# First modulation in quarters of the features instead of halves, with three projections begun beside it

## The chip, the cores and the metric

One Trainium2 chip, one of its cores. The metric is the device time of one execution, in microseconds (us). The engines of the core run side by side and wait for each other through semaphores: TensorE (PE) multiplies matrices, ScalarE (ACT) and VectorE (DVE) work on elements, GpSimd (POOL) does a few side jobs, and SyncE (SP) issues most of the transfers (DMA) from the chip's memory.

## The reference

Three transformer layers over 256 tokens of 1024 features, in float32. The part that matters here is the beginning of the first:

```
mod = (silu(c) @ w_ada + b_ada)          # 6 x 1024: shift1, scale1, gate1, shift2, scale2, gate2
h   = rms_norm(x, norm1_w) * (1 + scale1) + shift1
proj = h @ w_in                          # keys, queries, values of the delta rule, gates a and b, ...
qkv = silu(causal_conv(proj[:, :1536]))  # 4 taps, per feature
```

`c` is one vector, so `silu(c) @ w_ada` is a product of a vector with a matrix of 1024 x 6144. `h` needs its first two parts, shift1 and scale1: 2048 columns, 8 MB of weights. Behind `qkv` stand the gated delta rule, window attention, the output projection, a gated feed-forward layer and two more layers.

## The kernel before

Activations lie with the features on the 128 partitions: `x`, `norm_tmp` and the pair `h_hi`, `h_lo` have 8 pieces ("k", contraction steps) of 128 features by 256 tokens. To keep float32 precision, each operand of a product is split into a high part (ACT, `hi`, L669 and `first_highs`, L718) and a low part (DVE, `lo`, L1072 and `first_lows`, L1185), and every product is three: high x high, high x low, low x high (`three`, L1715). Weights come as blocks of 1 MB, 256 output columns each, from one stream in the order in which they are used, through a ring of three raw buffers (`load`, L548): block n + 3 is fetched when the low part of block n has been made. The column blocks w0 to w5 are the two halves of the keys, of the queries and of the values; a block is 8 steps x 2 tiles x 3 = 48 products.

The first modulation runs in two halves of 512 features each (loop lines 1864 to 1892 on PE). For each half SP loads four matrices of 1 MB (`load_ada`, L557, pieces of 2 KB in memory): scale rows in two, shift rows in two, the last of which comes as two transfers. `ada` (L1827) multiplies a column of `silu(c)` with four 512-wide rows at once in four groups of 32 columns of the PE array; ACT copies the result (`mod_rows_copy`, L713); `row_sums` (L1837) turns each 128 of it into a column and adds over the partitions. The last quarter of each half goes by `last_columns` (L1848) in 64 products of one output column. DVE then makes scale and shift (`first_scales` L1129, `first_shifts` L1135), scales the rows (`first_scaled` L1121), ACT makes `h_hi` (`h_high`, L696), DVE `h_lo` (`first_low` L1125). Beside the loads of the second half PE does steps 0 to 3 of w0 and w1 (`column_half`, L1721, with FIRST_WEIGHTS = 2, L30). `warm` (L1859) issues products of zeros that nobody reads, which fill the PE while it waits.

After the second half `project` (L1917) finishes w0, then come the 24 products for the gates a and b (lines 1928 to 1932, into bank B[0]), the rest of w1, and w2 to w5 whole. For each block ACT copies the product into `pad` (L759) when the convolution of the block before is done, DVE convolves it (L1229 to L1247) and ACT applies silu (`feature`, L743), whose result the next convolution waits for. DVE's order in this loop (L1218) is `lo(w + 2)`, then the convolution of w; ACT's (L750) is `hi(w + 2)`, the copy of w, `feature(w - 1)`. Every engine works strictly in the order in which its program is written, so a wait holds up all that stands behind it.

Later, from L1287 on, DVE alternates between splitting w8 to w10, the sums of the next modulation (`accumulate`) and reading the banks that PE fills (`row_scale`, L1301); PE may fill a bank again when DVE has read it (`before`, L1948).

Of the kernel before, what the change touches and what calls it, by code (L numbers as in the profile page):

```python
# [29 lines left out]
FIRST_WEIGHTS = 2  # L30
# [138 lines left out]
class Semaphores:  # L169


    def __init__(self, new):
# [3 lines left out]
        self.ada_rest_landed = new("ada_rest_landed")  # L176
# [143 lines left out]
def build(nc, stream, x_in, consts_in, vectors_in, gab_in, t5_onehot, t5_log, rel_bias, out):  # L320
    t5_scratch = nc.dram_tensor("t5_scratch", (16, 384), F32, kind="Internal")
    with ExitStack() as ctx:
        s = Semaphores(lambda name: ctx.enter_context(nc.semaphore(name)))
        ada_landed = [ctx.enter_context(nc.semaphore(f"ada_landed{i}")) for i in range(4)]
# [79 lines left out]
        mod_rows = [[inv_b[:, 1024 * i + 512 * u:1024 * i + 512 * u + 512] for u in range(2)] for i in range(2)]  # L404
        ada_raw = [flat(AT), flat(qkT), flat(X), flat(kqb[:, 0:8, :])]
# [140 lines left out]
        @block.sync  # L546
        def _(sp):
            def load(i):  # L548
                if i >= RING:
                    kind, n, _ = LOADS[i - RING]  # L550
                    if kind == "w":
                        sp.wait_ge(s.lo_ready, n + 1)
                    else:
                        sp.wait_ge(s.mod_accumulated, n - MOD_START[1] + 1)
                sp.dma_start(raw[:, i % RING, :], stream[LOADS[i][2]]).then_inc(raw_landed[i % RING], 16)

            def load_ada(half, i):  # L557
                if half and i < 3:
                    sp.wait_ge(s.ada_used, i + 1)
                elif half:  # L560
                    sp.wait_ge(s.rows_summed, 2)
                k, c = 4 * (i % 2), 512 * half + (D if i < 2 else 0)
                rows = ada_raw[i].rearrange("p (k c) -> p k c", k=4)
                if i < 3:
                    sp.dma_start(rows, stream[k:k + 4, :, c:c + 512].rearrange("k p c -> p k c")).then_inc(ada_landed[i], 16)
                    return
                for two, landed in enumerate((ada_landed[3], s.ada_rest_landed)):
                    sp.dma_start(rows[:, 2 * two:2 * two + 2, :],
                                 stream[k + 2 * two:k + 2 * two + 2, :, c:c + 512].rearrange("k p c -> p k c")).then_inc(landed, 16)
# [3 lines left out]
            for i in range(4):  # L573
                load_ada(0, i)
            load(0)
            load(1)
            for i in range(4):
                load_ada(1, i)
            sp.wait_ge(ada_landed[2], 32)
            for i in range(2, len(LOADS)):  # L580
# [73 lines left out]
        def _(act):  # L654
# [58 lines left out]
            def mod_rows_copy(half, u):  # L713

                act.wait_ge(s.ada_used, 3 * half + (3 if u else 2))
                act.activation(mod_rows[half][u], B[u][:, :], ACT.Copy).then_inc(s.rows_copied, 1)
# [12 lines left out]
            first_highs(0, (1,))  # L729
            h_high(0, range(2, 4))  # L730
            first_highs(0, (2, 3))
            first_highs(1, (0, 1))
            act.wait_ge(s.gab_loaded, 16)
            act.activation(gab_wh[:, :], gab_w[:, :], ACT.Copy).then_inc(s.gab_hi, 1)
            first_highs(1, (2, 3))
            mod_rows_copy(1, 0)
            mod_rows_copy(1, 1)
            h_high(0, range(4, KD))
# [11 lines left out]
            for w in range(6):  # L750
                hi(w + 2)
# [10 lines left out]
                if w == 0:  # L762
                    act.wait_ge(s.gab_product, 1)
                    act.activation(gabT, B[0][0:16, 0:T], ACT.Copy).then_inc(s.gab_copied, 1)
# [299 lines left out]
        def _(dve):  # L1064
# [64 lines left out]
            def first_scales(half):  # L1129
                c, at = slice(4 * half, 4 * half + 4), 480 + 8 * half  # L1130
                dve.wait_ge(s.rows_summed, 2 * half + 1)
                link(dve.tensor_tensor(a1[:, c], STAT[:, at:at + 4], b_scale[:, c], ALU.add))
                dve.tensor_tensor(a1[:, c], a1[:, c], vecs("norm1")[:, c], ALU.mult).then_inc(s.mod_ready, 1)

            def first_shifts(half):  # L1135
                c, at = slice(4 * half, 4 * half + 4), 484 + 8 * half
                dve.wait_ge(s.rows_summed, 2 * half + 2)
                dve.tensor_tensor(mods[:, c], STAT[:, at:at + 4], vecs("b_ada")[:, c], ALU.add).then_inc(s.mod_ready, 1)
                dve.wait_ge(s.mod_ready, 2 * half + 2)

            def h_parts_2():
                dve.wait_ge(s.rstd_ready, 2)
                dve.wait_ge(s.mod_ready, 6)
# [17 lines left out]
            def residual(last):  # L1161

                for m in range(KD):
# [4 lines left out]
                    if m == 0:  # L1168
                        dve.wait_ge(s.mod_ready, 5)
# [12 lines left out]
            for k in range(KD):  # L1182
                dve.tensor_tensor(nt[:, k, :], x[:, k, :], B[3][:, 256:512], ALU.mult).then_inc(s.x_scaled, 1)
# [16 lines left out]
            first_scaled(2)  # L1200
            first_scaled(3)
            first_lows(0, (1,))
            first_low(2)
            first_low(3)
            first_lows(0, (2, 3))
            first_lows(1, (0, 1, 2, 3))
            dve.wait_ge(s.gab_hi, 1)
            dve.tensor_tensor(gab_wl[:, :], gab_w[:, :], gab_wh[:, :], ALU.subtract).then_inc(s.gab_lo, 1)
            first_scales(1)
            first_shifts(1)  # L1210
            for k in range(4, KD):
                first_scaled(k)
                if k > 4:
                    first_low(k - 1)
            first_low(KD - 1)


            for w in range(6):  # L1218
# [5 lines left out]
                lo(w + 2)  # L1224
# [479 lines left out]
        def _(pe):  # L1704
# [16 lines left out]
            def column_half(w, bank, ks):  # L1721

                if ks[0] == 4:
                    pe.wait_ge(s.lo_ready, w + 1)
                wh = high_of(w)
                wl = low_of(w)
                for k in ks:
                    if k in (0, 2):
                        pe.wait_ge(s.first_lo, 3 * w + k // 2 + 1)
                    pe.wait_ge(s.h_lo_ready, k + 1)  # L1730
# [96 lines left out]
            def ada(half, i):  # L1827

                pe.wait_ge(ada_landed[i], 16 * (half + 1))
                if half and i % 2 == 0:  # L1830
                    pe.wait_ge(s.rows_copied, 1 + i // 2)
                for k in range(4):
                    ins = mm(B[i // 2][32 * k:32 * k + 32, :], c_columns[:, 4 * (i % 2) + k, :],
                             ada_raw[i][:, 512 * k:512 * k + 512], i % 2 == 0, i > 0)
                ins.then_inc(s.ada_used, 1)

            def row_sums(half, u):  # L1837

                pe.wait_ge(s.rows_copied, 2 * half + u + 1)
                if half + u:  # L1840
                    pe.wait_ge(s.mod_ready, 2 * half + u)
                for j in range(4):
                    at = 480 + 8 * half + 4 * u + j
                    ins = by_halves(STAT[:, at:at + 1], mod_rows[half][u][:, P * j:P * j + P], ones, j == 0, u == 0)
                if u == 0:
                    ins.then_inc(s.rows_summed, 1)

            def last_columns(half):  # L1848

                for k in range(4):  # L1850
                    if k % 2 == 0:
                        pe.wait_ge(s.ada_rest_landed if k else ada_landed[3], 16 * (half + 1))
                    for j in range(4):
                        at = 484 + 8 * half + j
                        ins = by_halves(STAT[:, at:at + 1], ada_raw[3][:, 512 * k + P * j:512 * k + P * j + P],
                                        c_act[:, 4 + k:5 + k], False, k == 3)
                ins.then_inc(s.rows_summed, 1)
# [13 lines left out]
            warm(4)  # L1871
            ada(0, 1)
            warm(3)
            row_sums(0, 0)
            warm(2)
            ada(0, 2)
            warm(3)
            row_sums(0, 1)
            warm(1)
            last_columns(0)  # L1880
            warm(6)
            column_half(0, A[0], range(4))
            ada(1, 0)
            column_half(1, A[1], range(2))
            ada(1, 1)
            column_half(1, A[1], range(2, 4))
            row_sums(1, 0)
            ada(1, 2)
            warm(3)
            row_sums(1, 1)  # L1890
            last_columns(1)
            warm(4)
# [24 lines left out]
            def project(w, halfway=None):  # L1917
                wait_bank(w)
                if w < 2:
                    column_half(w, A[w], range(4, KD))  # L1920
# [3 lines left out]
            for w in range(6):  # L1924
                project(w)
                if w == 0:

                    pe.wait_ge(s.gab_lo, 1)
                    for k in range(KD):
                        a, b = gab_wh[:, 16 * k:16 * k + 16], gab_wl[:, 16 * k:16 * k + 16]  # L1930
                        ins = three(B[0][0:16, 0:T], a, b, h_hi[:, k, :], h_lo[:, k, :], k == 0, k == KD - 1)
                    ins.then_inc(s.gab_product, 1)
# [386 lines left out]
            def spread(f, half):  # L2319

                if f == 0:
                    pe.wait_ge(s.mod_ready, 7)
# [234 lines left out]
```

## Time and profile before

| | us |
|---|---|
| median of 3 runs | 991.35 (990.08 to 991.51) |
| profiled execution | 990.9 |
| its span | 989.1 |
| PE busy | 978.5 (99% of the span) |
| DVE busy | 607.8 (61%) |
| ACT busy | 476.8 (48%) |

The busy time of PE counts a product from its start to its modelled end, so waits of PE that are shorter than a product's way through the array hardly show in it. The page's chain of work that ended last leads back from the end of the kernel to its start, and 98% of it is PE.

### The profile page before, as it was taken

What the parts mean: (1) busy time and instruction counts of PE and PEld (TensorE: products, weight loads), DVE (VectorE), ACT (ScalarE), POOL (GpSimd) and SP (SyncE); (2) the same over time, 40 slices, a digit from 0 to 9 for tenths busy, and PEclk for the clock granted to TensorE, in tenths of its full rate; (3) what the DMA queues carried; (4) which work ended last, traced back from release to release, by engine and by line L of the source; (5) the groups of instructions that cost most, each with busy time, mean ns of one, the idle gap of its engine ahead of it and who ended that gap; (6) DMA issues with size and microseconds to landing.
All of it is one profiled execution on the core that took longest, in us unless ns stands there. A gap on an engine that the chain in (4) does not pass through costs nothing.

```text
span 989.1 us, 15628 instructions
## 1 busy us (share of the span) xinstructions
PE 978.5 (99%) x6703; PEld 847.0 (86%) x6703; DVE 607.8 (61%) x750; ACT 476.8 (48%) x640; POOL 36.8 (4%) x37
## 2 busy tenths in 40 slices
PE   9999999999999999999999999999999999999998
PEld 6799988978888888999888888889999888888886
DVE  2589988775665454787754545365876663545444
ACT  3485277454343435533354344446655563435343
POOL 0000560010000000000000000000000000000000
PEclk9999999999999999999999999999999999999999
DMA  9757324775767354446544645454643435454621
GB/s 345 284 191 259 122 87 151 270 243 214 278 217 285 132 211 172 171 171 214 211 145 153 216 167 206 177 191 153 226 156 130 139 144 185 180 204 166 216 86 43
DMA packets 31588, 185.70 MB, mean 188 GB/s; under 512 B 3040, under 2 KB 5536, under 8 KB 10784
## 3 DMA queue, kind: packets, MB, share of 16 engines
q1 hardware_dynamic: 29984, 180.37, 51.0%
q0 software_dynamic: 832, 3.17, 1.0%
q8 instruction: 53, 0.87, 0.3%
q10 hardware_dynamic: 704, 1.17, 0.3%
q14 instruction: 15, 0.12, 0.0%
HBM read 183.62 MB, written 1.07 MB: 187 GB/s over the span
## 4 chain that ended last, share of the span: by engine, by line
PE 98%; DVE 1%; ACT 0%; issue 0%; POOL 0%; DVEq 0%; POOLq 0%
PE bank L1706 51%; PE acc L1706 43%; PE bank L2308 1%; PE bank L2086 1%; PE bank L1802 0%; PE acc L1802 0%; PE acc L2086 0%; PE bank L2166 0%; PE bank L1979 0%; DVE inv_b L1391 0%; DVE norm_tmp L1511 0%; DVE silu_and_hid L1510 0%; DVE inv_b L1384 0%; PE acc L2316 0%; DVE X_inv L1435 0%
## 5 line engine op out<-in xcount | busy, mean ns | idle before, releaser
L1075 DVE TENSOR_TENSOR w_lo<-raw,w_hi 128x2048 fp32r<-128x2048 f32 x144 | 326.9, 2289 | 146.2 <-ACT w_hi L675 146.1
L1706 PE MATMUL bank<-w_hi,h_parts 128*128 128x512 f32 x1056 | 333.5, 391 | 1.3 <-DVE h_parts L1152 1.3
L675 ACT ACTIVATE w_hi<-raw 128x2048 fp32r<-128x2048 f32 x144 | 271.5, 1909 | 102.3 <-PE acc L1706 70.9
L1706 PEld LDWEIGHTS bank<-w_hi,h_parts 128*128 128x128 f32 x1056 | 198.2, 188 | 44.6 <-issue 2.0
L1706 PE MATMUL bank<-w_lo,h_parts 128*128 128x512 f32 x528 | 205.5, 389 | 0.0
L1706 PE MATMUL acc<-h_parts,w_hi 128*128 128x256 f32 x928 | 170.8, 286 | 0.6 <-DVE h_parts L1127 0.6
L1706 PEld LDWEIGHTS acc<-h_parts,w_hi 128*128 128x128 f32 x928 | 143.5, 190 | 5.3 <-issue 3.3
L1706 PE MATMUL acc<-h_parts,w_lo 128*128 128x256 f32 x464 | 131.2, 283 | 0.0
L1706 PE MATMUL acc<-w_hi,o_hi 128*128 128x512 f32 x296 | 119.1, 402 | 0.0
L1706 PEld LDWEIGHTS bank<-w_lo,h_parts 128*128 128x128 f32 x528 | 99.2, 188 | 19.8
L1706 PE MATMUL acc<-w_hi,o_lo 128*128 128x512 f32 x296 | 115.6, 391 | 0.0
L1706 PE MATMUL acc<-w_lo,o_hi 128*128 128x512 f32 x296 | 115.6, 390 | 0.0
L1706 PEld LDWEIGHTS acc<-h_parts,w_lo 128*128 128x128 f32 x464 | 88.0, 190 | 0.0
L927 ACT ACTIVATE silu_and_hid<-bank,rms 128x256 f32<-128x256 f32 x44 | 20.9, 475 | 105.2 <-PE bank L1706 105.2
L1550 DVE TENSOR_TENSOR o_lo<-bank,o_hi 128x512 fp32r<-128x512 f32 x33 | 22.8, 691 | 76.0 <-ACT o_hi L932 76.0
L1706 PEld LDWEIGHTS acc<-w_hi,o_lo 128*128 128x128 f32 x296 | 55.6, 188 | 12.4
L1706 PEld LDWEIGHTS acc<-w_hi,o_hi 128*128 128x128 f32 x296 | 55.6, 188 | 10.9 <-issue 0.2
L1706 PEld LDWEIGHTS acc<-w_lo,o_hi 128*128 128x128 f32 x296 | 55.7, 188 | 10.5
L932 ACT ACTIVATE o_hi<-bank 128x512 fp32r<-128x512 f32 x33 | 19.8, 599 | 75.2 <-PE bank L2308 75.2
L1542 DVE SCALAR_TENSOR_TENSOR silu_and_hid<-bank,rms,silu_and_hid 128x256 f32<-128x256 f32 x44 | 21.2, 481 | 36.6 <-ACT silu_and_hid L927 36.6
L1706 PE MATMUL bank<-h_parts,w_hi 128*128 128x256 f32 x192 | 34.7, 283 | 0.3 <-DVE h_parts L1520 0.3
L1706 PEld LDWEIGHTS bank<-h_parts,w_hi 128*128 128x128 f32 x192 | 29.4, 188 | 0.7 <-DVE h_parts L1520 0.5
(370 smaller groups left out, 993.3 us busy)
## 6 DMA issues: line engine op xcount, KB each, us to landing
raw<-stream SPq DMA_DIRECT2D x162, 1024.0 KB, 5.1
AT<-stream SPq DMA_DIRECT2D x2, 1024.0 KB, 11.8
qkT<-stream SPq DMA_DIRECT2D x2, 1024.0 KB, 13.0
X_inv<-stream SPq DMA_DIRECT2D x2, 1024.0 KB, 14.2
keys_queries<-stream SPq DMA_DIRECT2D x4, 512.0 KB, 12.4
t_tables<-t_scratch POOLq DMA_DIRECT2D x1, 2048.0 KB, 10.2
x_res<-x_in SPq DMA_DIRECT2D x2, 512.0 KB, 5.2
t_tables<-t_scratch POOLq DMA_DIRECT2D x1, 1024.0 KB, 12.4
```

The source lines that it names most:

```text
L675: act.activation(high_of(w), raw_of(r), ACT.Copy).then_inc(s.hi_ready, 1)
L927: act.activation(sg[:, T * t:T * t + T], B[t][:, 0:256], ACT.Silu, scale=rms[:, t:t + 1] if f else 1.0).then_inc(s.silu_ready, 1)
L932: act.activation(hid_parts(j)[0].rearrange("p a b -> p (a b)"), B[2][:, :], ACT.Copy).then_inc(s.hid_hi_ready, 1)
L1075: dve.tensor_tensor(low_of(w), raw_of(weight_load(w)), high_of(w), ALU.subtract).then_inc(s.lo_ready, 1)
L1542: dve.scalar_tensor_tensor(out=o, in0=up, scalar=rms[:, t:t + 1], in1=gate, op0=ALU.mult, op1=ALU.mult).then_inc(s.hid_ready, 1)
L1550: dve.tensor_tensor(low.rearrange("p a b -> p (a b)"), B[2][:, :], high.rearrange("p a b -> p (a b)"), ALU.subtract).then_inc(s.hid_lo_rea ...
L1706: return pe.matmul(o, l, r, start=start, stop=stop, skip_group_check=True)
L2086: ins = pe.transpose(bank[hh][:, P * i:P * i + P], sc[:, hh, P * i:P * i + P], perm)
L2308: ins = pe.transpose(B[2][:, T * i + P * t:T * i + P * t + P], hid[:, T * t + P * i:T * t + P * i + P], ident)
```

## The change

`load_ada(q, u)` now loads, for each quarter q of 256 features, one matrix of scales (u = 0) and one of shifts (u = 1), each 1 MB in pieces of 1 KB. Blocks w0, w1 and w2 are loaded behind quarters 0, 1 and 2. `ada(q, u)` takes all eight contraction steps in one go, 256 wide; `last_columns` is gone. `row_sums` handles two columns a call, and there are eight calls in place of four. The scales, shifts, scaled rows and the two parts of `h` are made two steps a quarter. `column_part` replaces `column_half`: between the quarters PE does steps 0 to 5 of w0, w1 and w2, and the same steps of the gate factors (`gab_part`, now into B[3]); steps 6 and 7 of each are left for `project`. The loops of ACT and DVE skip `hi(2)` and `lo(2)`, which `first_highs` and `first_lows` do in quarter 2. Only four of the eight `norm_tmp` rows are made ahead of the first scale. The `warm` products go from 26 to 21 after the first 20. The core of the diff:

```diff
-FIRST_WEIGHTS = 2
+FIRST_WEIGHTS = 3
+QUARTERS = 4
...
+            def load_ada(q, u):
+                i = 2 * q + u
+                if i >= 4:
+                    sp.wait_ge(s.ada_used, i - 3)
+                c = 256 * q + (0 if u else D)
+                sp.dma_start(ada_raw[i].rearrange("p (k c) -> p k c", k=KD),
+                             stream[0:KD, :, c:c + 256].rearrange("k p c -> p k c")).then_inc(ada_landed[i], 16)
...
+            for q in range(QUARTERS):
+                load_ada(q, 0)
+                load_ada(q, 1)
+                if q < FIRST_WEIGHTS:
+                    load(q)
...
+            for q in range(1, QUARTERS):
+                mod_rows_copy(q, 0)
+                mod_rows_copy(q, 1)
+                h_high(0, range(2 * q, 2 * q + 2))
+                if q < FIRST_WEIGHTS:
+                    first_highs(q, (0, 1, 2, 3))
...
+            for q in range(1, QUARTERS):
+                first_scales(q)
+                first_shifts(q)
+                first_scaled(2 * q)
+                first_scaled(2 * q + 1)
+                first_low(2 * q)
+                first_low(2 * q + 1)
+                if q < FIRST_WEIGHTS:
+                    first_lows(q, (0, 1, 2, 3))
...
+            def ada(q, u):
+                pe.wait_ge(ada_landed[2 * q + u], 16)
+                if q:
+                    pe.wait_ge(s.rows_copied, 2 * (q - 1) + u + 1)
+                for k in range(KD):
+                    at = 32 * (k % 4)
+                    ins = mm(B[u][at:at + 32, 0:256], c_columns[:, k, :], ada_raw[2 * q + u][:, 256 * k:256 * k + 256], k < 4, k >= 4)
+                ins.then_inc(s.ada_used, 1)
...
             ada(0, 0)
             rstd(0)
-            warm(4)
+            warm(2)
+            row_sums(0, 0)
+            warm(1)
             ada(0, 1)
...
+            warm(2)
             row_sums(0, 1)
             warm(6)
-            column_half(0, A[0], range(4))
+            column_part(0, range(0, 2))
             ada(1, 0)
+            gab_part(range(0, 2))
+            row_sums(1, 0)
+            warm(2)
             ada(1, 1)
+            warm(2)
             row_sums(1, 1)
+            warm(6)
+            column_part(0, range(2, 4))
+            column_part(1, range(0, 2))
+            ada(2, 0)
+            column_part(1, range(2, 4))
+            row_sums(2, 0)
+            ada(2, 1)
+            gab_part(range(2, 4))
+            row_sums(2, 1)
+            column_part(0, range(4, 6))
+            column_part(1, range(4, 6))
+            ada(3, 0)
+            column_part(2, range(0, 3))
+            row_sums(3, 0)
+            ada(3, 1)
+            column_part(2, range(3, 4))
+            row_sums(3, 1)
+            column_part(2, range(4, 6))
+            gab_part(range(4, 6))
```

## Rows read from the trace of the kernel before

**Rows 1.** The page, part 4: the chain that ended last, shares of the span.
```profile
PE 98%; DVE 1%; ACT 0%; issue 0%; POOL 0%; DVEq 0%; POOLq 0%
```

**Rows 2.** The chain in order of time, 41 to 78 us: start us, us, what.
```profile
41.11 3.09 PE acc L1706 x24
44.20 3.56 PE bank L1706 x26
...
51.02 17.28 PE acc L1706 x144
...
68.87 8.65 PE acc L1706 x72
```

**Rows 3.** Windows: from:to, length, busy (x count) by engine, PEclk, DMA share, GB/s.
```profile
20.00:22.00 2.00, 2.00 (x64) 2.00 (x60) 0.00 (x0) 0.00 (x0) 0.00 (x0) 0.82 0.99 414
...
20.00:30.00 10.00, 10.00 (x102) 8.58 (x98) 7.49 (x17) 5.83 (x13) 0.00 (x0) 0.66 1.02 390
```

**Rows 4.** The transfers' view of 1.6 to 2.1, 12 to 13, 36 to 41, 970 to 989 us.
```profile
AT<-stream SPq DMA_DIRECT2D x1, 1024.0 KB, 8.7
...
DMA packets 196, 0.38 MB, mean 383 GB/s; under 512 B 9, under 2 KB 9, under 8 KB 196
...
DMA packets 293, 2.14 MB, mean 428 GB/s; under 512 B 32, under 2 KB 32, under 8 KB 32
...
GB/s 0 0 0 0 34 0 0 0 0 0 0 0 0 0 0 0 0 0 0 0 0 0 0 0 0 0 0 0 0 0 207 278 289 283 196 286 284 292 93 0
DMA packets 2113, 1.07 MB, mean 56 GB/s; under 512 B 64, under 2 KB 2112, under 8 KB 2112
```

**Rows 5.** Timeline, PE, 16 to 40 us: start us, us, engine, line, operation.
```profile
24.83 0.63 PE L1706 MATMUL acc<-h_parts,w_hi 128*128 128x256 f32 x2
...
29.22 1.07 PE L1706 MATMUL bank<-AT,c_columns 128*32 128x512 f32 x8
...
36.90 0.63 PE L1706 MATMUL bank<-consts,inv_b 128*64 128x1 f32 x16
37.38 2.01 PE L1706 MATMUL bank<-c_act_sb,keys_queries 128*64 128x1 f32 x64
```

**Rows 6.** Timeline, DVE and ACT, 16 to 40 us.
```profile
22.21 0.16 DVE L1138 TENSOR_TENSOR mods<-bank,vec 128x4 f32<-128x4 f32 x1 [5.60 <-PE bank L1706]
...
36.14 0.60 ACT L716 ACTIVATE inv_b<-bank 128x512 f32<-128x512 f32 x1 [2.58 <-PE bank L1706]
...
39.44 0.16 DVE L1138 TENSOR_TENSOR mods<-bank,vec 128x4 f32<-128x4 f32 x1 [3.96 <-PE bank L1706]
```

**Rows 7.** Timeline, DVE, then ACT, 44 to 68 us.
```profile
44.24 2.29 DVE L1075 TENSOR_TENSOR w_lo<-raw,w_hi 128x2048 fp32r<-128x2048 f32 x1 [1.38 <-ACT w_hi L675]
...
46.98 2.46 DVE L1240 SCALAR_TENSOR_TENSOR XT<-inv_p,vec,XT 128x256 f32<-128x256 f32 x6
...
53.92 0.62 DVE L1233 TENSOR_SCALAR XT<-inv_p,vec 128x256 f32<-128x256 f32 x2 [2.28 <-ACT keys_queries L745]
...
57.34 2.28 DVE L1075 TENSOR_TENSOR w_lo<-raw,w_hi 128x2048 fp32r<-128x2048 f32 x1
...
65.16 2.29 DVE L1075 TENSOR_TENSOR w_lo<-raw,w_hi 128x2048 fp32r<-128x2048 f32 x1 [1.31 <-ACT w_hi L675]
...
44.23 0.60 ACT L759 ACTIVATE inv_p<-acc 128x512 f32<-128x512 f32 x1
...
50.84 0.60 ACT L759 ACTIVATE inv_p<-acc 128x512 f32<-128x512 f32 x1 [1.61 <-PE acc L1706]
51.46 1.28 ACT L745 ACT_TABLE_LOAD   x1
```

**Rows 8.** Timeline, DVE, then PE, 89 to 100 us.
```profile
89.57 0.69 DVE L1303 TENSOR_TENSOR keys_queries<-keys_queries,bank 128x512 f32<-128x512 f32 x1 [0.15 <-PE bank L1706]
...
98.65 0.68 DVE L1303 TENSOR_TENSOR keys_queries<-keys_queries,bank 128x512 f32<-128x512 f32 x1
...
98.98 1.09 PE L1979 MATMUL bank<-consts,inv_p 128*128 128x128 f32 x8
```

More of the change, by code:

```diff
@@ L323, in build @@
         s = Semaphores(lambda name: ctx.enter_context(nc.semaphore(name)))
-        ada_landed = [ctx.enter_context(nc.semaphore(f"ada_landed{i}")) for i in range(4)]
+        ada_landed = [ctx.enter_context(nc.semaphore(f"ada_landed{i}")) for i in range(2 * QUARTERS)]
         raw_landed = [ctx.enter_context(nc.semaphore(f"raw_landed{i}")) for i in range(RING)]
@@ L555, in load @@
                 sp.dma_start(raw[:, i % RING, :], stream[LOADS[i][2]]).then_inc(raw_landed[i % RING], 16)
[L557 to L569, printed above, removed]
+            def load_ada(q, u):
[5 more added lines that the diff above has]
+                             stream[0:KD, :, c:c + 256].rearrange("k p c -> p k c")).then_inc(ada_landed[i], 16)
             sp.dma_start(x[:, 0:4, :], x_in[:, 0:4, :]).then_inc(s.x_lower_loaded, 16)
             sp.dma_start(x[:, 4:8, :], x_in[:, 4:8, :]).then_inc(s.x_upper_loaded, 16)
[L573 to L580, printed above, removed]
+            for q in range(QUARTERS):
[3 more added lines that the diff above has]
+                    load(q)
+            for i in range(FIRST_WEIGHTS, len(LOADS)):
                 load(i)
@@ L711, in _, with mod_rows_copy @@
             root(0)
-            def mod_rows_copy(half, u):
-                act.wait_ge(s.ada_used, 3 * half + (3 if u else 2))
-                act.activation(mod_rows[half][u], B[u][:, :], ACT.Copy).then_inc(s.rows_copied, 1)
+            def mod_rows_copy(q, u):
+                act.wait_ge(s.ada_used, 2 * q + u + 1)
+                act.activation(mod_rows[q][u], B[u][:, 0:256], ACT.Copy).then_inc(s.rows_copied, 1)
             def first_highs(w, quarters):
@@ L1181, in _, with normed_rows @@
             dve.wait_ge(s.rstd_ready, 1)
-            for k in range(KD):
-                dve.tensor_tensor(nt[:, k, :], x[:, k, :], B[3][:, 256:512], ALU.mult).then_inc(s.x_scaled, 1)
+            def normed_rows(ks):
+                for k in ks:
+                    dve.tensor_tensor(nt[:, k, :], x[:, k, :], B[3][:, 256:512], ALU.mult).then_inc(s.x_scaled, 1)
+            normed_rows(range(4))
             def first_lows(w, quarters):
@@ L1199, in _ @@
             first_low(1)
[L1200 to L1206, printed above, removed]
+            normed_rows(range(4, KD))
             dve.wait_ge(s.gab_hi, 1)
             dve.tensor_tensor(gab_wl[:, :], gab_w[:, :], gab_wh[:, :], ALU.subtract).then_inc(s.gab_lo, 1)
[L1209 to L1215, printed above, removed]
+            first_lows(0, (1, 2, 3))
+            for q in range(1, QUARTERS):
[7 more added lines that the diff above has]
+                    first_lows(q, (0, 1, 2, 3))
             for w in range(6):
@@ L1825, in _ @@
             two = lambda b: b[:, :].rearrange("p (a b) -> p a b", a=2)
[L1827 to L1834, printed above, removed]
-                ins.then_inc(s.ada_used, 1)
@@ new lines, in row_sums, with gab_part @@
+            def row_sums(q, u):
+                pe.wait_ge(s.rows_copied, 2 * q + u + 1)
+                if q + u:
+                    pe.wait_ge(s.mod_ready, 2 * q + u)
+                for j in range(2):
+                    at = 480 + 4 * q + 2 * u + j
+                    ins = by_halves(STAT[:, at:at + 1], mod_rows[q][u][:, P * j:P * j + P], ones, True, True)
+                ins.then_inc(s.rows_summed, 1)
+            def gab_part(ks):
+                pe.wait_ge(s.x_scaled, KD)
+                pe.wait_ge(s.gab_lo, 1)
+                for k in ks:
+                    pe.wait_ge(s.h_lo_ready, k + 1)
+                    a, b = gab_wh[:, 16 * k:16 * k + 16], gab_wl[:, 16 * k:16 * k + 16]
+                    ins = three(B[3][0:16, 0:T], a, b, h_hi[:, k, :], h_lo[:, k, :], k == 0, k == KD - 1)
+                if ks[-1] == KD - 1:
+                    ins.then_inc(s.gab_product, 1)
@@ L1918, in project @@
                 wait_bank(w)
-                if w < 2:
-                    column_half(w, A[w], range(4, KD))
+                if w < FIRST_WEIGHTS:
+                    column_part(w, range(6, KD))
                 else:
@@ L1926, in _ @@
                 if w == 0:
[L1928 to L1932, printed above, removed]
+                    gab_part(range(6, KD))
                     pe.wait_ge(s.t5_loaded, 48)
```

85 lines of the change are left out of this document (25 added, 60 removed).

## The prediction

> **What bounds the kernel now.** I read the page's chain first: 98% of it is PE [rows 1], so a change counts only by how it moves the products' order in time. Then that chain in order of time. From 41.11 us on PE runs without a pause through w0, the gates, w1 and w2 [rows 2], so the start costs what stands before 41.11, and the products left behind it. Next the windows: in 20 to 30 us the mean clock is 0.66, which is 6.8 us at half of 2.4 GHz (1.2 GHz), begun at about 21.3, and the engines that move data are full, at 390 GB/s [rows 3]. Last the timelines of PE, ACT and DVE, for durations and for what DVE and ACT do behind the first projections.
>
> The profiled execution took 990.9 us, its span 989.1; the median of three is 991.35. The sum is made on 990.9, then 0.45 is added.
>
> **The transfers.** The first matrix was issued at 1.65 and landed 8.7 later, at 10.35 [rows 4]. Pieces of 2 KB run at 383 GB/s, blocks in longer pieces at 428 [rows 4]: 2.7 and 2.45 us a MB. No row has pieces of 1 KB. The bounds are 383 GB/s, and the final stores, whose 2048 packets under 2 KB ran at about 285 GB/s [rows 4]: 2.7 to 3.7 us. I take 3.1, the middle leaning to the loads, because the row of stores is another direction. The first matrix then lands at 10.8, and the rest in the order of issue: 13.9, w0 16.4, quarter 1 at 19.5 and 22.6, w1 25.1, quarter 2 at 28.2 and 31.3, w2 33.8, quarter 3 at 36.9 and 40.0. SP's new waits are on buffers that PE has left long before (quarter 3 needs the product of 21 us), so I cost them at nothing; behind them only later weights stand. If they did hold, each us would move 36.9 by one.
>
> The Trainium skill ("DMA: Bandwidth & Descriptors", Specifications) asks for 512 B or more for line rate, by which 1 KB pieces would go as 2 KB ones and Tq below would be about 0.3 lower. The stores here, at 285 against 383 GB/s for loads in 2 KB, speak against it.
>
> **Parts on PE.** `ada` of four 512-wide rows takes 1.07 [rows 5]. Eight 256-wide calls in two rounds of four have the same columns: I take 1.05, with bounds of 1.0 and 1.3 (the columns alone, and twice as many weight loads). `row_sums` of 16 records takes 0.63, 0.56 without its tail [rows 5]; eight records 0.3. `last_columns`, 2.0 each [rows 5], goes twice. Products of 256 columns cost 0.129 each in the first pieces (3.09 / 24) and 0.12 in whole blocks (17.28 / 144) [rows 2]. A part of 12 is 1.55, six gate products are 0.7.
>
> From the last sum to the first product of the next two steps: 39.44 to 41.11, 1.67 [rows 2, 6]; in the first quarter, where the weight parts come between, 22.21 to 24.83, 2.6 [rows 5, 6]. From the end of `ada` to its sums: ACT's copy took 0.60 for 512 columns [rows 6], I take 0.4 for 256 and 0.2 of ways, 0.6.
>
> **The sum.** Quarter 0: `ada` 13.9 to 14.95, sums from 15.55 to 15.85, first product 18.45 (w0 landed at 16.4). Quarter 1: 18.45 + 1.55 + 1.05 + 0.7 + 0.3 + 0.4 of zeros = 22.45; the shift matrix lands at 22.6: + 1.05 + 0.6 + 0.3 + 1.7 = 26.25. The `warm` products lie in these waits. Quarter 2: from here PE has work all along: 1.55 x 2 + 1.05 + 1.6 + 0.3 + 1.05 + 0.7 + 0.3 = 8.1, to 34.35, then a wait of 1.7 with nothing in it: 36.05. Quarter 3: 1.55 x 2 + 1.05 + 2.35 + 0.3 + 1.05 + 0.8 + 0.3 + 1.55 + 0.7 = 11.2, to 47.25 (loads landed at 36.9 and 40.0; the last `h` is ready before). Call this Tq.
>
> What is left on PE up to the end of w2: 15.7 before (41.11 to 56.8, a third of the 17.28 behind 51.02, [rows 2]) less 78 products moved ahead, 9.4: 6.3. PE alone would end w2 at 53.5, 3.3 earlier than before.
>
> But DVE and ACT get their work later. Before, step 7 of w0 ended at 44.20 [rows 2]; now at 47.25 + 1.55 = 48.8, 4.6 later. ACT's copy and DVE's first convolution start only then. Before, from 44.20 to the start of the second convolution, 53.92, passed 9.7 [rows 7]: in it `lo(2)` pushed the first convolution from 44.85 to 46.45, gone now, 1.6; and the copy at 50.84 waited 1.4 for PE's end of w1, though the convolution had ended at 49.44 [rows 7], gone too. With 0.2 of small gaps 3.2 is won back, and 1.4 of lateness is left: the second convolution starts at 55.3, `lo(4)` ends at 61.0 (before 59.6), `lo(5)` at 68.85 (before 67.45) [rows 7].
>
> So w3 can't start at 53.5: `lo(3)` is queued on DVE behind the first convolution (0.65 + 2.95 + 2.3 behind 48.8), 54.75, against 56.8 before: 2.0 ahead. w4 waits for `lo(4)`, 61.0 against 62.5: 1.5 ahead. w5 waits for `lo(5)`, 68.85 against 68.87: nothing ahead [rows 2]. DVE stays 1.4 late. Up to the fourth bank read, 98.65, DVE has short waits for PE of which the first is 0.15 (three such, 0.5 together) [rows 8]; they go. It comes 0.9 late, and PE's transposes at 98.98 (the second of them refills the bank just read) were right behind it [rows 8]. PE is then 0.9 late and has no long slack to take it back. 990.9 + 0.9 + 0.45 = 992.25; I say 992.2. Because the chain through DVE decides, every us of Tq moves the end by one; break-even is Tq = 46.35.
>
> Other edits at nothing: the gate factors in B[3] (free after the rows are normed; the wait for `x_scaled` is met at 20.3), the rows normed in two parts (under the wait for w0's low part; uncovered 1.4), semaphore counts.
>
> **Rivals.** *The clock falls.* Before it fell after a stretch with 64 products of one column and few `warm`; it cost 6.8 us at half speed. For: the wait at 34.35 to 36.05 has no `warm`, and 0.3 of one-column products ahead. Against: the similar wait before 41.11 did not cost the clock, and most of 31 to 34 is dense. Price: 6.8 us at half in a stretch that PE bounds, 3.4: 995.6. The Trainium skill ("TensorE: Matmul & The Clock Gate", Part 1) says that activity releases a throttle which is the default; the trace agrees, with 0.66 in 20 to 30 us.
>
> *Small pieces are slow.* At 285 GB/s a MB takes 3.7; quarter 1 is complete four matrices on, 2.4 later, at 25.0, and Tq is 49.5 or so. Price 2.3: 994.5. For: the row of the stores. Against: another direction.
>
> *PE's lead is kept*, faster: the place is w3, 3.3 ahead. If DVE and ACT keep up, the end is 3.3 earlier: 988.0. It decides from where the second convolution starts by 52 or so. Against: that needs Tq near 43 or shorter DVE work; the rows have neither. For: my Tq is a sum of some thirty terms, and `ada` and the first stage could each be shorter.
>
> *The quarters don't overlap as written* (loads held back by SP): it would show like the second rival, and I count it there.
>
> **How the numbers follow.** About 2.0 us either way (0.2%) is what can be told from no change. My forecast, 0.6, own range 990.0 to 994.0 (Tq 45.2 to 49.2): 0.48 same, 0.10 slower, 0.02 faster. Clock falls 0.15 (0.14 slower, 0.01 same); slow pieces 0.12 (0.11 slower, 0.01 same); lead kept 0.13 (0.11 faster, 0.02 same). Together faster 0.13, same 0.52, slower 0.35. The range leaves out a part of each outer case: 989.3 to 995.6.
>
> **What would show it.** The last matrix landing near 40; the first `h` of quarter 1 used at 26.3, of quarter 2 at 36; step 6 of w0 at about 47.3; waits of PE for `w_lo` ahead of w3, w4 and w5; the second convolution at 55.3; the fourth bank read near 99.6; PEclk 1.00 from start to 60. Wrong if w3 starts behind 56.8 or the convolution before 53.9; if PEclk shows a half in 20 to 45, the first rival holds.

## The result, and the profile after

The changed kernel took 996.34 us (median of 6 runs, 994.95 to 998.9), the kernel before 991.37 in the runs beside it: ratio 1.0048, interval 1.0031 to 1.0065. A second set of eight runs gave 995.66, ratio 1.0036 [1.0019, 1.0054]. It is slower, by more than the 0.2% that can be told, and above the top of the range given (994.0). The profiled execution took 995.09, its span 993.3.

The page's chain that ended last, shares of the span by engine (before: 98% PE, [rows 1]):

```profile
PE 93%; DVE 3%; DMA 2%; ACT 1%; SPq 1%; issue 1%; DVEq 0%; ACTq 0%
```

PE no longer holds the chain alone: a transfer enters at the start, DVE and ACT between w0 and w5. In order of time (start us, us, what):

```profile
7.74 15.46 DMA keys_queries<-stream
23.20 0.04 issue
23.24 1.07 PE bank L1701 x16
...
27.02 3.08 PE acc L1701 x24
...
36.90 3.08 PE acc L1701 x24
...
48.17 1.43 PE acc L1701 x12
49.63 0.61 ACT inv_p L752
50.26 0.62 DVE XT L1228 x2
...
67.21 2.31 DVE w_lo L1068
69.65 10.30 PE acc L1701 x72
79.94 1.03 PE bank L1701 x32
...
151.83 4.53 PE bank L1701 x64
```

The shift matrix of quarter 1 lands at 23.2. The first products of quarters 1 and 2 follow at 27.02 and 36.90, step 6 of w0 at 48.17. From its end the chain goes over ACT's copy and DVE to the low part of w5 at 67.21, and w5 starts at 69.65, against 68.87 before [rows 2]. The same 72 products then take 10.30 in place of 8.65 [rows 2], 1.65 more, and 64 products at 151.83 take 4.53 where the kernel before took 2.90 for them, 1.63 more. The work is the same; the clock isn't. The windows (from:to, length, busy us and count of PE, PEld, DVE, ACT, POOL, then PEclk, DMA share, GB/s):

```profile
30.00:40.00 10.00, 8.29 (x95) 6.44 (x98) 4.48 (x11) 3.59 (x8) 0.00 (x0) 1.00 1.06 375
...
50.00:60.00 10.00, 8.97 (x69) 7.75 (x66) 9.14 (x21) 8.28 (x10) 0.00 (x0) 1.00 0.57 193
60.00:70.00 10.00, 8.32 (x70) 8.09 (x69) 8.39 (x18) 8.60 (x13) 0.68 (x1) 1.00 0.32 107
70.00:80.00 10.00, 10.00 (x76) 9.87 (x76) 9.97 (x20) 7.73 (x9) 0.00 (x0) 0.83 0.62 211
...
150.00:160.00 10.00, 8.79 (x124) 8.35 (x123) 7.43 (x14) 6.50 (x21) 1.91 (x3) 0.83 0.24 80
```

PEclk 0.83 over ten us is 3.4 us at 1.2 GHz, with half of that lost. The fall at 20 to 30 us [rows 3] is gone. Two new ones have come, at 70.6 and at 152.5. The first is right behind the empty wait for w5, in a stretch (50 to 70) in which PE is no longer full. The second is behind a wait of 1.2 us for `X_inv`, which the kernel before has as well, without a fall behind it; in PE's timeline, before and after:

```profile
149.41 1.09 PE L1706 MATMUL bank<-consts,X_inv 128*64 128x128 f32 x16 [1.22 <-DVE X_inv L1435]
...
151.83 1.37 PE L1701 MATMUL bank<-consts,X_inv 128*64 128x128 f32 x16 [1.21 <-DVE X_inv L1430]
```

The new empty waits, by the view of waits of PE, 12 to 72 us (who waited for whom, us in total, times, longest):

```profile
PE acc L1701 <- DVE w_lo L1068: 2.7, 3, 1.3
PE acc L1701 <- DVE h_parts L1120: 1.7, 1, 1.7
PE acc L1701 <- DVE w_lo L1187: 1.4, 1, 1.4
```

DVE's timeline, for the second convolution, `lo(5)` and the fourth bank read (start us, us, engine, line, operation, [idle before]):

```profile
55.99 0.62 DVE L1228 TENSOR_SCALAR XT<-inv_p,vec 128x256 f32<-128x256 f32 x2 [0.54 <-ACT keys_queries L737]
...
67.21 2.29 DVE L1068 TENSOR_TENSOR w_lo<-raw,w_hi 128x2048 fp32r<-128x2048 f32 x1 [1.30 <-ACT w_hi L668]
...
101.08 0.68 DVE L1298 TENSOR_TENSOR keys_queries<-keys_queries,bank 128x512 f32<-128x512 f32 x1
```

DVE is 2.05 to 2.07 later than before at both of the first two (55.99 against 53.92, 67.21 against 65.16, [rows 7]), and 2.43 at the bank read (98.65, [rows 8]).

**How the runs spread.** Each run comes with its mean granted clock, and the time follows it: a mean 0.001 lower is 2 us of the span at half clock, which costs 1 us at most. In the profiled runs half clock comes in stretches of 3.4 us, worth 1.7 at most each. So a median holds two things: the time without such stretches ahead of the last microseconds (runs at a mean clock of 0.999 or 1.000), and what they add.

| kernel | runs | median us | mean clock | at 0.999 or more: runs, median us |
|---|---|---|---|---|
| before, all calls below | 92 | 991.3 | 0.9954 | 13, 989.5 |
| changed, both sets | 14 | 996.3 | 0.9946 | 0 (three at 0.998: 993.8, 993.8, 994.1) |
| e1_fill_waits | 12 | 995.85 | 0.9958 | 2, 992.8 |
| e8_fill_one_wait | 11 | 995.4 | 0.9960 | 2, 992.7 |
| e5_fill_all_waits | 12 | 993.19 | 0.9978 | 7, 992.7 |
| e2_two_blocks | 12 | 993.05 | 0.9972 | 4, 991.7 |
| e3_short_chain | 12 | 993.56 | 0.9952 | 1, 990.25 |
| e7_short_chain_filled | 12 | 994.39 | 0.9957 | 3, 990.4 |
| e4_small_pieces | 12 | 992.27 | 0.9955 | 0 |
| e6_before_early_fill | 6 | 997.8 | 0.9925 | 0 |

### The profile page after: what moved, and what is told of

Same layout as the page of the kernel before. It is cut to its first block, busy times and chain, and to the rows that moved or that the text cites. A ratio compares the mean times of both kernels' runs of the same rounds, so it can differ in the third digit from the quotient of the medians.

```text
span 993.3 us, 15568 instructions
## 1 busy us (share of the span) xinstructions
PE 977.3 (98%) x6650; PEld 845.5 (85%) x6650; DVE 609.2 (61%) x759; ACT 478.3 (48%) x647; POOL 36.7 (4%) x37
## 3 DMA queue, kind: packets, MB, share of 16 engines
HBM read 183.62 MB, written 1.07 MB: 186 GB/s over the span
## 4 chain that ended last, share of the span: by engine, by line
PE 93%; DVE 3%; DMA 2%; ACT 1%; SPq 1%; issue 1%; DVEq 0%; ACTq 0%
PE bank L1701 50%; PE acc L1701 40%; DMA keys_queries<-stream 2%; PE bank L2311 1%; DVE XT L1235 1%; PE bank L2089 1%; SPq L555 0%; PE bank L1798 0%; DVE w_lo L1068 0%; PE acc L1798 0%; PE acc L2089 0%; SPq L563 0%; PE bank L2169 0%; ACT w_hi L668 0%; DVE XT L1228 0%
## 5 line engine op out<-in xcount | busy, mean ns | idle before, releaser
L920 ACT ACTIVATE silu_and_hid<-bank,rms 128x256 f32<-128x256 f32 x44 | 20.9, 475 | 105.3 <-PE bank L1701 105.3
(370 smaller groups left out, 994.4 us busy)
## 6 DMA issues: line engine op xcount, KB each, us to landing
keys_queries<-stream SPq DMA_DIRECT2D x2, 1024.0 KB, 14.7
```

What stands on the lines that cost most here:

```text
L920: act.activation(sg[:, T * t:T * t + T], B[t][:, 0:256], ACT.Silu, scale=rms[:, t:t + 1] if f else 1.0).then_inc(s.silu_ready, 1)
```

## The experiments

My theory after the result: PE's empty waits, at 35 and ahead of w3 to w5, let the clock fall, and the chain over ACT and DVE behind the later w0 costs a smaller part. Rivals: the chain alone; the third block; the small pieces.

### e1_fill_waits: the changed kernel with zeros in the waits ahead of w3, w4, w5

```diff
+WAIT_FILL = {3: 5, 4: 1, 5: 8}
...
+                if w in WAIT_FILL:
+                    warm(WAIT_FILL[w], A[w % 4])
```

> The changed kernel with 5, 1 and 8 more products of zeros ahead of w3, w4 and w5, in the banks that these then overwrite, so that PE is not idle while it waits for w_lo. Theory (the end is late by 0.8 us of waiting for DVE and ACT, and by 1.7 us for each interval of 3.4 us at the lower clock that PE's idle waits bring on): no lower clock between 60 and 80 us, w5 still starts at about 69.7, w6's second half at about 79.3 instead of 81.0, and the median about 1.5 us under the changed kernel's, near 994.5; mean clock of the runs up by about 0.002. Rival (the lower clock has nothing to do with these waits): the clock falls there as before and the median stays at 996.3 or rises by up to 1.

995.85, ratio 1.0048 [1.0032, 1.0064]: no gain. Its windows show why:

```profile
30.00:40.00 10.00, 8.29 (x88) 6.47 (x88) 4.59 (x13) 3.59 (x8) 0.00 (x0) 0.93 1.06 376
40.00:50.00 10.00, 10.00 (x99) 8.36 (x99) 2.37 (x9) 1.51 (x4) 0.00 (x0) 0.90 0.59 242
```

The filled stretch, 60 to 80, stays at 1.00. But a fall lies at 38.6 to 42.0, behind the wait of quarter 2, and the 24 products there (37.86) take 4.60 in place of 3.08. Another lies at 11.3 to 14.7, ahead of all waits that the change brought; quarter 1's first products start at 27.98 for 27.02. With one kind of wait filled, falls still came in other places.

### e2_two_blocks: the changed kernel with the third early block undone

```diff
-FIRST_WEIGHTS = 3
+FIRST_WEIGHTS = 2
...
-            column_part(2, range(0, 3))
...
-            column_part(2, range(3, 4))
+            warm(2)
...
-            column_part(2, range(4, 6))
+            warm(3)
```

> The changed kernel with the third block undone: w0 and w1 alone are begun beside the quarters, w2 is loaded, split and multiplied behind them as before; products of zeros stand in two of the three places. Theory of the chain through DVE: step 6 of w0 comes about 3 us earlier (near 45), but lo(2) stands ahead of the first convolution again (1.6), so w5 starts near 68.5 and, without a fall of the clock, the end is within 0.5 us of the kernel before. Rival (PE's own work decides, and the third block is a gain): slower than the changed kernel by 1 to 3 us.

993.05, ratio 1.0013 [0.9999, 1.0027]; its runs without a fall are at 991.7, 1.0 under the 992.7 of the three versions that add only fills (e1, e5, e8). The early w2 therefore costs rather than gains: PE's lead from it can't be used (w3 waits for DVE), and it pushes step 6 of w0 later. The wait for `h` of quarter 2 is still there, and so is a fall behind it in the profiled run. From the chain of waits, then PE's timeline:

```profile
37.71 4.60 PE acc L1701 x24
...
47.92 0.48 PE L1701 MATMUL acc<-h_parts,w_hi 128*128 128x256 f32 x2
```

The second line is step 6 of w0. In e1, whose profile has falls at the same two places (11.3 and 38.6), it starts at 50.64, 2.7 later.

### e3_short_chain: the changed kernel with less on the chain behind w0

Steps 4 and 5 of the gate factors go behind w0; ACT's table for silu is loaded before it is needed; `hi(5)` stands ahead of ACT's wait for the gates' logarithm.

```diff
+            act.activation(root_tmp[:, :], ones, ACT.Silu)
...
-                if w + 2 >= FIRST_WEIGHTS:
+                if w + 2 >= FIRST_WEIGHTS and w != 3:
...
+                    hi(5)
...
-            gab_part(range(4, 6))
...
-                    gab_part(range(6, KD))
+                    gab_part(range(4, KD))
```

> The changed kernel with its chain through ACT and DVE shortened: the gate products of steps 4 and 5 go behind the last part of w0 (0.7 us earlier start of the first convolution), the silu table is loaded by a dummy activation in ACT's idle time at 47 us (1.3 us off feature(0)), and hi(5) is made before the wait for the gates' logarithm (1.3 us off lo(5)). Theory: second convolution at about 55.0 instead of 56.0, lo(5) done by about 68.0, w5 starts 1.3 to 2 us earlier than in the changed kernel (69.65), shorter idle waits of PE and fewer falls of the clock; median 993 to 994.5, 2 to 3 us under the changed kernel. Rival (the chain doesn't decide, the first stage or the later clock does): no more than 0.5 us faster.

993.56, ratio 1.0021 [1.0007, 1.0035]; its one run at 0.999 took 990.25, and the three of e7, with the same chain, 990.3 to 991.0: 2.3 under the 992.7 of the versions with the long chain. DVE's timeline of the profiled run, with a fall at 38.1 that made its w0 1.0 later (first convolution at 51.26, not 50.26):

```profile
56.48 0.61 DVE L1230 TENSOR_SCALAR XT<-inv_p,vec 128x256 f32<-128x256 f32 x2
...
66.83 2.28 DVE L1070 TENSOR_TENSOR w_lo<-raw,w_hi 128x2048 fp32r<-128x2048 f32 x1
...
99.77 0.68 DVE L1300 TENSOR_TENSOR keys_queries<-keys_queries,bank 128x512 f32<-128x512 f32 x1
```

From the first convolution to the second are 5.22 in place of 5.73, to `lo(5)` 15.57 in place of 16.95, and the bank read comes at 99.77, 0.6 ahead of e5's 100.40 (below) though its first convolution was 1.1 later (50.14 in e5). Shortening the chain moves the end. Whether the same edits would also speed up the kernel before was not run, so the 2.3 isn't a measure of what the change itself put on this chain; e5 (below) measures that.

### e4_small_pieces: the kernel before with its first matrices in 1 KB pieces

```diff
-                    sp.dma_start(rows, stream[k:k + 4, :, c:c + 512]...).then_inc(ada_landed[i], 16)
+                    for b in (0, 256):
+                        sp.dma_start(rows[:, :, b:b + 256],
+                                     stream[k:k + 4, :, c + b:c + b + 256]...).then_inc(ada_landed[i], 16)
```

The same for the matrix in two transfers, with the waits counted to match.

> The kernel before, with the same bytes of the first modulation loaded in pieces of 1 KB, by twice as many transfers. If small pieces cost what the changed kernel's rate shows (about 3.0 us a MB against 2.7), the last matrix lands about 2.4 us later (8 x 0.3), and since PE waits for it behind quarter-filled time, the first projection of the second half starts 1 to 2.5 us later than 41.11, the end likewise: 992.5 to 994. If they cost nothing: 991.4, unchanged.

992.27, ratio 1.0006 [0.9991, 1.0021]; the interval holds 1. In the chain of waits w2 starts 1.05 later than before (51.02, [rows 2]), and 0.74 later than in b2 (51.33, below), whose profile has its falls at the same places as this one (22.7 and 39.8):

```profile
32.02 1.06 PE bank L1709 x8
...
52.07 3.99 PE acc L1709 x32
```

so small pieces cost some 0.7 us of the start where all loads go in them (twice the transfers are in that, too); the medians alone can't tell it from nothing.

### a2_changed_again: the changed kernel itself, a second time

> The changed kernel itself, for more of its runs with their clocks. By the sum of its first profile (0.8 us late at w5 against a kernel before that had itself an interval of 6.8 us at the lower clock, and 1.65 us for each of two intervals of 3.4 us): the runs spread by about 1.7 us for each interval, the span of those at a mean clock of 0.998 or more is near 990 (the kernel before: 987.5), the median again near 996, the median clock 0.993 against 0.996. Rival (a constant loss, no clock in it): spread no wider than 1 us, and all runs near 995 to 996.

995.66, ratio 1.0036 [1.0019, 1.0054]. Three runs at clock 0.998 took 993.8 to 994.1, two at 0.991 took 997.9. This profiled run had half clock from 37.9, 72.0 and 154.0: behind the wait for quarter 2's `h`, behind the waits for `w_lo`, and behind the wait for `X_inv` that is not new.

### e5_fill_all_waits: e1, and six zeros ahead of quarter 2's products too

```diff
+            warm(6)
             column_part(0, range(4, 6))
```

> The changed kernel with products of zeros in all four of its new empty waits: 6 ahead of steps 4 and 5 of w0 (PE idle 34.8 to 36.9), and 5, 1 and 8 ahead of w3, w4 and w5. Theory of the clock: hardly a fall before 140 us, median 992.5 to 994, 2 to 3.5 us under the changed kernel, clock of the median run 0.996 or more. Rival (falls come from somewhere else, as e1 hints with falls at 11 and 39 us): median 995 to 996 as in e1.

993.19, ratio 1.0017 [1.0005, 1.0029]. Seven of twelve runs stand at a mean clock of 0.999 or 1.000; in the changed kernel without them it was none of fourteen. The profiled one (992.77, span 990.9) is the changed kernel's order without a fall before the last microseconds. Windows:

```profile
30.00:40.00 10.00, 9.87 (x100) 7.46 (x104) 4.48 (x11) 3.59 (x8) 0.00 (x0) 1.00 1.06 375
...
50.00:60.00 10.00, 10.00 (x73) 8.67 (x72) 9.25 (x21) 8.29 (x10) 0.00 (x0) 1.00 0.58 193
60.00:70.00 10.00, 10.00 (x76) 9.36 (x76) 8.38 (x18) 8.60 (x13) 0.68 (x1) 1.00 0.33 109
70.00:80.00 10.00, 10.00 (x107) 9.84 (x106) 9.97 (x19) 7.75 (x9) 0.00 (x0) 1.00 0.62 210
```

DVE's timeline:

```profile
55.87 0.62 DVE L1229 TENSOR_SCALAR XT<-inv_p,vec 128x256 f32<-128x256 f32 x2 [0.54 <-ACT keys_queries L738]
...
67.09 2.29 DVE L1069 TENSOR_TENSOR w_lo<-raw,w_hi 128x2048 fp32r<-128x2048 f32 x1 [1.30 <-ACT w_hi L669]
...
98.13 2.35 DVE L1086 SCALAR_TENSOR_TENSOR inv_b<-raw,c_act_sb,inv_b 128x2048 f32<-128x2048 f32 x1 [0.36 <-DMA raw<-stream]
100.40 0.68 DVE L1299 TENSOR_TENSOR keys_queries<-keys_queries,bank 128x512 f32<-128x512 f32 x1
```

The chain over DVE stands where it stood in the changed kernel (55.99, 67.21), so the zeros took nothing away from it and put nothing on it. The bank read is 1.75 later than before [rows 8], and the span 1.8 longer than the 989.1 of before. Nothing behind it changes this.

### e6_before_early_fill: the kernel before with one product of zeros ahead of each 16 of `last_columns`

A guess that the kernel before could be rid of its own fall in this way.

```diff
                 for k in range(4):
+                    warm(1)
                     if k % 2 == 0:
                         pe.wait_ge(s.ada_rest_landed if k else ada_landed[3], 16 * (half + 1))
```

> The kernel before with one product of zeros ahead of each of the four quarters of last_columns, in both halves, so that the stretch of one-column products ahead of the fall at 21.5 us is denser. It adds 0.9 us of PE in each half; in the second half that lies on the path. Theory: the fall at 21.5 goes in nearly all runs, worth up to 1.6 us a run, and the median is 991.0 to 991.8, with the lowest runs 0.9 later than those of before. Rival (one-column products have no part in it): 992.3, 0.9 slower in all runs.

997.8, ratio 1.0058 [1.004, 1.0075], 5.9 slower than before; neither the theory nor its rival (0.9 slower) holds. The second `last_columns` with its fills in the chain of waits:

```profile
38.82 0.56 PE bank L1706 x16
39.38 0.42 PE acc L1706
39.80 0.56 PE bank L1706 x16
40.37 0.43 PE acc L1706
...
43.34 5.58 PE acc L1706 x28
```

A lone product of zeros between short ones costs 0.42 (three in a row took 0.89 in the kernel before): 4 x 0.42 = 1.7 each time, and two of these, 3.4. The clock still fell, twice (from 22.9 for 6.8 us and from 43.4 for 3.4), and 28 products behind took 5.58.

### e7_short_chain_filled: e3, with fills

```diff
+WAIT_FILL = {3: 3, 5: 3}
...
+            warm(6)
             column_part(0, range(4, 6))
```

and the edits of e3.

> The changed kernel with the shortened chain of e3 and the filled waits (6 ahead of steps 4 and 5 of w0, 3 ahead of w3 and w5). Theory: both losses are gone but what is left at the bank reads near 100 us: clean runs as in e3 (span 988.4 at a clock of 0.999), and fewer disturbed ones; median 991.0 to 992.5. If only the chain counted, as in e3: 993.5.

994.39, ratio 1.001 [0.9996, 1.0025]. Three runs are at 990.3 to 991.0, seven at 994.4 to 995.0 with a mean clock of 0.992 to 0.994. The profiled run, one of these, had half clock at 11.6 to 18.5 and at 151.6 to 155.0: the first ahead of all waits of the change (e8 shows more of it), the second behind the wait for `X_inv`. So the fills aren't sure to help: they leave these two places as they are.

### e8_fill_one_wait: the changed kernel with only quarter 2's wait filled

```diff
+            warm(6)
             column_part(0, range(4, 6))
```

> The changed kernel with one edit: 6 products of zeros ahead of steps 4 and 5 of w0, where PE is otherwise idle from 34.8 to 36.9 us. e1 had the other three waits filled and gained nothing (995.85 against 995.66), e5 had all four filled and gained 2.5. Theory A (the wait at 35 us is the one that brings on the falls that count, in the first stage where PE is the bound): median near 993.5, at least 1.5 under the changed kernel. Theory B (the wait at 35 and the waits for w_lo each bring on their own falls): 994.5 to 995, and a profile may show an interval between 60 and 80 us.

995.4, ratio 1.0029 [1.0014, 1.0045], two of eleven runs at 0.999 or more. Windows:

```profile
10.00:20.00 10.00, 10.00 (x87) 5.91 (x85) 3.08 (x12) 2.00 (x7) 0.00 (x0) 0.66 1.07 366
...
70.00:80.00 10.00, 8.69 (x62) 8.62 (x61) 9.80 (x18) 7.89 (x8) 0.00 (x0) 0.83 0.51 152
```

The stretch behind quarter 2 is clean and the one behind w5's wait isn't: the reverse of e1. Falls come behind both kinds of waits. With both filled the median was 2.5 under the changed kernel's (e5 against a2); e8's interval overlaps both the changed kernel's and e5's, so what one fill alone gains isn't told.

The first line is a fall at 11.6 to 18.5, and it costs more than the later one. PE's timeline of this run, then of e5, then the chain of this run:

```profile
8.42 2.45 PE L1701 MATMUL bank<-consts,norm_tmp 128*64 128x1 f32 x64 [0.53 <-ACT norm_tmp L679]
...
8.95 2.03 PE L1702 MATMUL bank<-consts,norm_tmp 128*64 128x1 f32 x64
...
50.49 1.43 PE acc L1701 x12
```

Step 6 of w0 comes at 50.49, 2.4 behind e5's 48.05, though the fill stopped the fall at 38. Four of the twelve profiles have this early fall (e1, e2, e7, e8), all of versions of the changed kernel. In those four PE had first waited 0.5 to 0.7 us for ACT's `norm_tmp`, ahead of 64 one-column products, since the 20 products of zeros before them ended sooner; in the other eight it had waited 0.2 or less. None of the edits touches what runs before 11 us.

### b2_before_again: the kernel before itself

> The kernel before itself, for a profile at another moment of the clock's intervals. If the fall at 21.5 us cost the kernel before 1.6 us (its runs at a mean clock of 0.999 have a span of 987.5 against 989.1 in the profile), a profile without it has w2 starting near 49.4 instead of 51.02, and the loss of the changed kernel at equal clock is about 3 us, not 0.8 to 1.5. Rival (the fall was hidden under the loads): w2 starts at 51.0 with or without it, and the 1.6 us lie elsewhere, as at 145 to 150 us.

990.73, ratio 0.9993 [0.9982, 1.0004]. Windows, then chain:

```profile
20.00:30.00 10.00, 9.74 (x109) 7.80 (x108) 7.78 (x17) 5.83 (x13) 0.00 (x0) 0.83 1.03 392
...
40.00:50.00 10.00, 9.99 (x67) 8.60 (x68) 7.17 (x15) 5.41 (x6) 0.00 (x0) 0.84 0.55 197
```

```profile
40.01 4.49 PE acc L1706 x24
...
51.33 17.28 PE acc L1706 x144
```

The kernel before falls too, here at 22.7 and at 39.7, the second behind its own wait for `h`, in which zeros leave PE idle for 0.6 only, with 64 one-column products ahead. It lost 1.4 there (4.49 against 3.09, [rows 2]). w2 then starts at 51.33, much as in the trace that I predicted from. But the first fall ended after 3.4 us, at 26.1, where that trace has half clock up to 28.1, and the products of step 4 start at 40.01 for 41.11. So the longer fall was not hidden under the loads: the second half of it cost 1.1. Starts without any fall are seen only in the times: 989.5, where the first profiled run took 990.9.

No version was faster than the kernel before.

## Why the prediction was wrong, point by point

The forecast was 992.2 and the changed kernel took 996.3: 4.1 off. It divides in two.

**The step that failed: falls of the clock, which have no term in the sum, and with them its base.** I took the changed kernel to run at full clock. Without falls the long-chain versions stand at 992.7 (e1, e5, e8), and the changed kernel itself at 996.3, so falls cost it 3.6, some two stretches or more. The changed kernel has no run without a fall, so 992.7 is read from versions that add zeros only; its three runs at 0.998, one stretch each by their clock, are at 993.8 to 994.1, which fits. I charged none; the 0.45 that I added is what lay between the profiled time and the median. 3.2 of the 4.1 are this (3.6 - 0.45). In the rival "the clock falls" the mechanism was right, but I gave it 0.15, and only one place, the wait at 34.35 to 36.05. That place is real (half clock at 38 in four of the profiled runs: a2, e1, e2, e3), but a fall there costs 1.5 and not 3.4, and the waits for `w_lo`, which I had in the sum as PE's lead that isn't used, are more such places. I priced them in time of PE and not in clock. Two further places I did not have at all, the start at 11 us and the wait for `X_inv` at 150 us; neither is a wait that the change brought. The sign that I named, "PEclk 1.00 from start to 60", could not catch this: the first profile of the changed kernel meets it, with its falls at 70.6 and 152.5, and the second (a2) doesn't. Against the rival I brought the wait before 41.11, which "did not cost the clock": one trace, and b2 shows a fall at just that place. And the 0.66 in 20 to 30 us, which I took as agreement with a release by activity, shows little of that by itself: PE is busy in all ten of these us [rows 3], and what came ahead of the fall were 64 one-column products.

The same holds for the base. The 990.9 held a fall worth 1.4 (990.9 - 989.5; b2 shows 1.1 of it in a trace). My sum let it go, with no gain named, and so hid that the forecast order was already 2.3 above the kernel before at full clock (991.8 against 989.5). The measured gap of 5.0 is 3.2 without falls (992.7 - 989.5) and 1.8 from falls (3.6 against 1.8). The mean clock hardly differs, 0.9946 against 0.9954, which is 0.8 us at most of that 1.8. The rest must be the place: a fall costs what PE bounds there. The profiled run of before had 6.8 us at half clock beside the first loads and was 1.4 over 989.5. The changed kernel's had 6.8 us too: the stretch at 70.6 cost PE 1.65, of which DVE would have taken 1.0 anyway (bank read 101.08 against 100.40 in e5, so 0.7 net), the one at 152.5 the full 1.63; together 2.3, and e5's span of 990.9 plus 2.3 is the 993.3 of the changed kernel to 0.1. How the places are spread over the runs without a profile isn't shown.

The Trainium skill ("TensorE: Matmul & The Clock Gate", Part 1) says of the first, slow matmuls of a kernel that for modeling the ramp penalty is under 1% of a typical span. It says so of the start and not of falls later on. The falls measured here are of that size too, 3.6 of 993 us or 0.36%, but they are most of the 4.1 by which I was off.

**The start, Tq: right in kind, 0.9 too early.** `ada` took 1.07 (1.05 forecast), `row_sums` 0.33 on the chain (0.3). First products: 18.66, 27.02 and 36.90 where I had 18.45, 26.25 and 36.05; step 6 of w0 at 48.17 for 47.25. The matrix that quarter 1 waits for landed at 23.2, not 22.6, and that 0.6 carried through all that follows. Small pieces were as forecast: the changed kernel's transfers at 26 to 32 us, GB/s in 40 slices:

```profile
GB/s 355 355 341 335 362 348 348 355 335 348 355 362 341 335 348 348 355 355 341 335 355 355 635 280 382 464 423 403 403 403 457 348 464 403 560 382 328 492 273 266
```

about 350 up to 29.3, while pieces of 1 KB move, which is 3.0 us a MB (3.1 forecast); then 400 and more with a weight block. The Trainium skill ("DMA: Bandwidth & Descriptors", Specifications) has 512 B as enough for line rate; the trace doesn't agree, with 350 against 383 [rows 4] for 2 KB. I had put the effect of that rate on Tq at 0.3, and that is a slip: at 2.7 us a MB the same sum has its first product at 17.6, the shift matrix at 20.9, and all behind it 1.0 earlier, Tq near 46.25.

**DVE and ACT decide, PE's lead can't be used: right.** w3 started at 55.5, 1.3 ahead of before (2.0 forecast), and w5 had nothing ahead: 0.8 late. DVE's lateness was 2.05 and not 1.4. In e5, without a fall, it was 1.93 at `lo(5)`; on the way to the fourth bank read its short waits gave 0.5 back (0.5 forecast), and a new wait for a transfer took 0.36 of that again: 1.75 late, forecast 0.9. That is 0.85 of the 4.1. As forecast, nothing takes it back later: 1.75 at the bank read, 1.8 in the span. And e3 and e7 show the mechanism from the other side: 2.3 less without falls from edits to this chain alone.

**The rivals.** Small pieces slow: no; e4 puts them at some 0.7 us of the start, and the rate that I took (3.1 us a MB) had that in the sum. PE's lead kept: no, as the second convolution came at 55.99 and not by 52. Transfers held back by SP: no, the matrices landed in order, and quarter 3 waited for none.

**What stays open.** Where falls lie in runs without a profile, and so how much of the changed kernel's 3.6 its new waits bring: the fall at 11 us follows a wait of PE at 8 us in all four profiles that have it, and the fall near 152 us (after, a2, e3, e7) follows a wait that all twelve have. No run filled either place.

## What to carry to other kernels

Moving PE's work into a phase that feeds it late buys nothing if another engine's chain, here w0's end, ACT's copy and two convolutions, sets the next start: work out when that chain's first input comes, and keep it early, before filling PE with work of later blocks. Look at the mean granted clock of every run, compare kernels at equal clock, and take the cost of falls out of the base before adding to it. Each new empty wait of PE between dense work, even of one to two us, should be charged with a chance of up to 1.7 us. Filling one group of them (e1, e8) gave nothing that could be told from noise, and filling both (e5) gave 2.5; so find every place with a fall, in several profiles, before judging a fill.

## What the runs showed of the hardware that I had not expected

- Times of one kernel go in steps: those of e5 are 992.2 to 993.3 (seven) and 995.0 to 995.2 (five), with nothing between, and mean clocks of 0.999 or more and 0.994 to 0.996. A single time of this kernel tells little under 0.3%.
- The stretches at half clock lasted 3.4 or 6.8 us in all the profiled runs (but for one at the very end, which the end of the kernel cuts off), and cost PE 1.5 to 1.65 per 3.4 where PE bounds (24 products 4.60 for 3.08, 64 products 4.53 for 2.90, 72 products 10.30 for 8.65). Beside the first loads they cost less: 6.8 us at 11.6 cost 2.4.
- Waits of PE of 1.2 to 1.7 us with nothing in them had falls behind them in one run and not in the next, the same wait in the same kernel: behind the one at 35 us the clock fell in a2 and not in the first profile.
- A wait of 0.5 to 0.7 us at 8 us, followed by 64 one-column products, had a fall at 11.2 to 11.6 behind it in all four profiles that have it, and none of the other eight fell there.
- Pieces of 1 KB move at about 350 GB/s, against 383 for 2 KB.
- A lone 512-wide product of zeros between one-column products cost 0.42, and in e6's profile did not keep the clock up.
